# Retention heads by tokens: group norm along the free axis, samples read from split old states

## What is computed

```
S_new = g * S_old + k^T v            # per head and sample: 256 x 512, stored
o     = q S_new                      # prompt: (decayed scores) v
o     = (o - mean(o)) * rsqrt(var(o) + eps) * gn_gain     # over the 512 channels of a token
ret   = (silu(gate) * o) @ w_ret_out
```

## Time and profile before

| | us |
|---|---|
| median of three runs | 2689.16 |
| lowest and highest | 2684.42, 2693.64 |
| the profiled execution | 2686.85 |
| its span, first to last instruction | 2685.0 |
| TensorE busy in it | 2561.6 |
| VectorE busy | 1396.5 |
| GpSimd busy | 1422.3 |
| ScalarE busy | 629.4 |

### The profile page before, as it was taken

The page is one execution under the profiler, slowest core; times in us unless marked ns, Lnnn a source line. Parts: engine busy times, 40 slices in busy tenths (PEclk is TensorE's granted clock), DMA queues, the critical chain, the costliest instruction groups (busy, mean ns, idle before and its releaser), DMA issues.

```text
span 2685.0 us, 52601 instructions
## 1 busy us (share of the span) xinstructions
PE 2561.6 (95%) x20388; PEld 2521.4 (94%) x20388; DVE 1396.5 (52%) x1480; ACT 629.4 (23%) x925; POOL 1422.3 (53%) x845
## 2 busy tenths in 40 slices
PE   6999999999999999999999999999999999999997
PEld 6999998989899999999988989999998999999997
DVE  7664636468864553133365455454787645430333
ACT  2312121216651121001112031312266411110111
POOL 4252535346666656566642525252566666566654
PEclk9999999999999999999998999999999999999999
DMA  4445353522233322332334353535222333223222
GB/s 152 166 126 169 122 173 115 172 69 93 75 92 95 91 88 90 89 94 87 95 125 162 118 159 122 165 122 173 81 83 77 97 89 93 87 86 102 86 87 86
DMA packets 113046, 298.97 MB, mean 111 GB/s; under 512 B 11680, under 2 KB 12448, under 8 KB 112864
## 3 DMA queue, kind: packets, MB, share of 16 engines
q1 hardware_dynamic: 60480, 199.78, 24.2%
q10 hardware_dynamic: 52384, 96.56, 10.6%
HBM read 255.92 MB, written 40.38 MB: 110 GB/s over the span
## 4 chain that ended last, share of the span: by engine, by line
PE 69%; DVE 12%; DVEq 6%; issue 3%; ACT 3%; DMA 3%; ACTq 2%; POOL 1%; POOLq 1%
PE proj L325 42%; PE aux L325 20%; PE aux L531 3%; DVE scratch L943 2%; DVEq L1087 2%; DMA scratch<-in_sret 2%; DVEq L946 1%; PE aux L522 1%; DVE scratch L896 1%; PE aux L512 1%; POOL w_low L313 1%; DMA out_ret_s<-scratch 1%; PE aux L479 1%; DVE scratch L901 1%; ACTq L1387 1%
## 5 line engine op out<-in xcount | busy, mean ns | idle before, releaser
L311 POOL TENSOR_SCALAR w_high<-w_raw 128x1024 fp32r<-128x1024 f32 (+3 forms) x420 | 442.1, 1053 | 1177.5 <-PE proj L325 946.5
L313 POOL TENSOR_TENSOR w_low<-w_raw,w_high 128x1024 fp32r<-128x1024 f32 (+3 forms) x420 | 979.7, 2333 | 62.2 <-issue 2.9
L325 PE MATMUL proj<-x_high,w_high 128*128 128x260 f32 x3072 | 637.7, 289 | 59.6 <-DVE scratch L791 15.8
L325 PE MATMUL proj<-x_high,w_low 128*128 128x260 f32 x3072 | 626.7, 286 | 0.0
L325 PE MATMUL proj<-x_low,w_high 128*128 128x260 f32 x3072 | 626.4, 286 | 0.0
L325 PEld LDWEIGHTS proj<-x_high,w_high 128*128 128x128 f32 x3072 | 483.0, 192 | 68.5 <-issue 28.0
L325 PEld LDWEIGHTS proj<-x_low,w_high 128*128 128x128 f32 x3072 | 481.8, 192 | 0.0
L325 PEld LDWEIGHTS proj<-x_high,w_low 128*128 128x128 f32 x3072 | 481.3, 192 | 0.0
L325 PE MATMUL proj<-split_scratch,w_high 128*128 128x260 f32 x2368 | 383.8, 284 | 4.7 <-DVE ret_acc L720 2.0
L325 PEld LDWEIGHTS proj<-split_scratch,w_high 128*128 128x128 f32 x2368 | 325.2, 189 | 7.7 <-DVE ret_acc L720 5.0
L325 PE MATMUL aux<-split_scratch,w_high 128*128 128x260 f32 x1632 | 265.3, 285 | 5.9 <-DVE scratch L978 3.8
(11 more groups left out here) (167 smaller groups left out, 2726.2 us busy)
## 6 DMA issues: line engine op xcount, KB each, us to landing
w_raw<-in_wstream SPq DMA_DIRECT2D x252, 512.0 KB, 3.5
scratch<-in_sret ACTq DMA_DIRECT2D x64, 512.0 KB, 6.4
out_ret_s<-scratch ACTq DMA_DIRECT2D x64, 512.0 KB, 6.3
w_raw<-in_wstream SPq DMA_DIRECT2D x72, 448.0 KB, 3.3
w_raw<-in_wstream SPq DMA_DIRECT2D x48, 384.0 KB, 3.1
scratch<-v_rows ACTq DMA_DIRECT2D x64, 256.0 KB, 4.9
w_raw<-in_wstream SPq DMA_DIRECT2D x48, 320.0 KB, 2.8
out_ret_p<-scratch ACTq DMA_DIRECT2D x8, 512.0 KB, 3.0
```

Of the source, the lines that this page charges most:

```text
L311: pool.tensor_scalar(WH[:, j, w], WR[:, j, w], 1.0, 0.0, ALU.mult, ALU.add)
L313: pool.tensor_tensor(WL[:, j, w], WR[:, j, w], WH[:, j, w].bitcast(F32), ALU.subtract).then_inc(s["w_split"], 1)
L325: m = pe.matmul(out, wt[:, w, blk * P:(blk + 1) * P], x[xi], start=first and n == 0, stop=last and n == 2)
```

## The change

Attention is computed by token blocks: the split scores are the stationary operand and the split values move, so that an output tile has 128 tokens on the partitions and 512 channels along the free axis. Group norm then works along the free axis: VectorE takes mean and variance with `bn_stats` and `bn_aggr` from the accumulator, ScalarE takes the root, VectorE the reciprocal and the shift on one column, ScalarE normalises. In the next head, after its two query units, TensorE transposes the normalised tiles back to channels (`turned_back`, 16 blocks and 4 small ones); VectorE multiplies them by the gate (`read_back`), ScalarE and VectorE split the result (`gated_out`, `og_split`). `og_split` moves from behind VectorE's first reading of a query tile to behind the rotation of k. The column sums are gone.

The samples are read out of their old states: ScalarE and VectorE split a state into SSH and SSL (`state_high`, `state_low`), and TensorE multiplies the split states, moving, by split query columns of which all but two are zero (`read_out`, 4 matmuls of 512 columns a sample), summing all samples in one accumulator. `samples` adds the parts, decays them and adds the q-k product times v. The first four read-outs stand behind the value units, the others between and behind the last gate units.

The gate tiles are in natural order, the four accumulators for these uses get another order with one semaphore each, the ring of v rows has four places instead of two, and in a first head the series moves ahead of and between the value tiles.

```diff
-                    rotate(0, QF, new_gain)
-                    rotate(KT, KF, lambda: low(QL, QF, QH, 1.0, 1))
+                    rotate(0, QF, lambda: None)
+                    if not first:
+                        read_back(hh - 1)
+                    dve.wait_ge(s["sfin_st"], hh * 16 + 16)
+                    rotate(KT, KF, q_parts)
                     ts(KSC[:], KF[:, :, SEQ:TOK], DK ** -0.5, None, ALU.mult)
-                    if not first:
+                    if first:
+                        series_begin()
+                        state_terms()
+                        state_low(0)
+                    else:
+                        new_gain()
                         for m_ in range(MT):
                             ret_add(tb, QK, m_)
...
+                def turned_back(hh):
+
+
+                    for use in TOKENS:
+                        pe.wait_ge(*turn(hh, use))
+                    for e in range(VT):
+                        if e == VT - 1:
+                            for c in range(VT):
+                                m = pe.transpose(AUX[:, BANK["OTS"], c * NS:(c + 1) * NS], NOS[:, c * P:(c + 1) * P],
+                                                 ID[0:NS, 0:NS])
+                            m.then_inc(s["aux_mm"], 1)
+                        aux_begin(hh, f"OT{e}")
+                        for t in range(TT):
+                            m = pe.transpose(aux(f"OT{e}")[:, t * P:(t + 1) * P], NO[:, t, e * P:(e + 1) * P], ID[:])
+                        m.then_inc(s["aux_mm"], 1)
...
+                    else:
+                        for i in range(KT):
+                            whole(ub, i, tb, i, XH, XL)
+                        turned_back(hh - 1)
+                    for i in range(KT, QK):
+                        whole(ub, i, tb, i, XH, XL)
                     if not first:
                         ret_out(hh, ub, QK, tb, QK)
...
+                        for d in range(KT):
+                            pe.wait_ge(s["s_low"], hh * (NS * KT) + (b * KT + d + 1))
+                            for n, part in enumerate((SSH, SSL)):
+                                m = pe.matmul(aux("RO", 2 * NS), QP[:, d, b, :], part[:, d, :],
+                                              start=b == d == n == 0, stop=b == NS - 1 and d == KT - 1 and n == 1)
+                            m.then_inc(s["ro_done"], 1)
...
                     gate(1)
-
-
-                    sample_out(0)
-                    gate(3, midway=lambda: sample_out(1))
-                    sample_out(2)
+                    gate(2)
+                    read_out(4)
+                    gate(3)
+                    read_out(5)
                     pe.wait_ge(s["kv_low"], hh * (2 * TT) + 2 * TT)
                     pe.wait_ge(s["st_low"], hh * TT + TT)
-                    for e in range(VT):
-                        attend(e)
-                        sample_out(3 + e)
+                    attend(3)
                     final_state(0)
-                    sample_out(NS - 1)
+                    read_out(6)
+                    attend(2)
+                    attend(1)
+                    read_out(7)
                     final_state(1)
-                    pe.wait_ge(s["gn_sum"], hh * 2 + 1)
-                    column_sums(tb, v0 + VT + T_MEAN, SUM)
-                    gate(2)
-                    pe.wait_ge(s["gn_sum"], hh * 2 + 2)
-                    column_sums(tb, v0 + VT + T_VAR, SUM)
+                    aux_begin(hh, "SEL")
+                    attend(0)
+                    samples()
...
+                    scaled(3)
+                    next_state(4)
+                    store_state(2)
+                    silu(1)
+                    scaled(4)
+                    next_state(5)
+                    store_state(3)
+                    scaled(5)
+                    next_state(6)
+                    state_high(4)
                     silu(2)
+                    store_state(4)
```

More of the change, by code:

```diff
@@ L241, in build @@
         v_ld = [sem(f"vb_loaded{j}") for j in range(VRING)]
+        a_free = [sem(f"aux_free{j}") for j in range(BANKS)]
         r_free = [sem(f"ring_free{j}") for j in range(RING)]
@@ L260, in freed, with turn, aux @@
             return r_free[n % RING], layer * USES[n % RING] + (n // RING + 2)
+        def turn(hh, use):
+            return a_free[BANK[use]], hh * BANK_USES[BANK[use]] + (TURN[use] + 2)
+        def aux(use, rows=P):
+            return AUX[0:rows, BANK[use], :]
         def slot(idx):
@@ L399, in spread @@
                 return q
[L401 to L406, removed]
             def norm_sums(outs, signal):
@@ L418, in _ @@
             pe.sem_inc(s["w_used"], 2)
-            for done in r_free:
+            for done in r_free + a_free:
                 pe.sem_inc(done, 1)
@@ L442, in x_early, with aux_begin @@
                 def x_early(t):
-                    whole(ub0, B_X_EARLY + t, tb0, C_X_EARLY + t, XH, XL,
-                          variances=(layer + 1) * HEADS if t == 1 else None)
+                    whole(ub0, B_X_EARLY + t, tb0, C_X_EARLY + t, XH, XL)
+                def aux_begin(hh, use):
+                    done, count = turn(hh, use)
+                    pe.wait_ge(done, count - 1)
+                def turned_back(hh):
[11 more added lines that the diff above has]
+                        m.then_inc(s["aux_mm"], 1)
                 def one_head(head, first):
@@ L482, in one_head @@
                         m.then_inc(s["aux_mm"], 1)
+                    aux_begin(hh, "QK")
+                    for d in range(KT):
+                        m = pe.matmul(aux("QK", NS)[:, 0:NS], KSC[:, d, :], QF[:, d, SEQ:TOK],
+                                      start=d == 0, stop=d == KT - 1)
+                    m.then_inc(s["aux_mm"], 1)
                     for i in range(TT // 2):
-                        aux_begin(N_TK + i)
+                        aux_begin(hh, f"TK{i}")
                         for j in range(2):
@@ L564, in _ @@
                     one_head(head, False)
-                for t in range(X_EARLY):
-                    x_early(t)
+                x_early(0)
+                turned_back((layer + 1) * HEADS - 1)
+                x_early(1)
                 ret_out((layer + 1) * HEADS, ub0, B_X_EARLY + X_EARLY, tb0, C_X_EARLY + X_EARLY)
```

393 lines of the change are left out of this document (227 added, 166 removed).

## The result

The changed kernel takes 2764.3 us (median of four runs, 2760.33 to 2766.02) against 2686.79 for the kernel before (also four): ratio 1.0301, 95% interval 1.0278 to 1.0325, slower (these two medians alone give 1.0289). The forecast was 2765 in 2718 to 2798. The profiled execution took 2766.02, its span is 2764.2, 79.2 more than before.

What follows compares the result with a forecast made beforehand. TensorE, busy 95% of the span, was taken as the bound. Work and waits saved were outweighed by new stops: two layers of a first head +11.1, three later heads +9.1 each and layer end +0.5, +78 on 2686.85, gave 2765, range 2718 to 2798.

Steps and rivals of the forecast that it cites:

- Stop 1: Turn back after the query units: fourth transposed block waits for VectorE's read behind the query's second rotation; 1.8 of wait.
- Stop 2: Output product after the last key unit waits for VectorE's late split of the gated output: 3.85 plus 1.0, 4.9.
- first heads' read-out 0: In a layer's first head, read-out 0 waits for VectorE's lambda series and convolution terms: 5.7, and 1.5 of clock.
- stop 4: Sample 4's read-out, between third and fourth gate units, waits for its state's ring slot: 10.0, plus 1.5 of clock.
- stop 3: A transposed value block, moved to the first key transposes' bank, waits for VectorE's two subtractions: 0.9.
- smaller stops: State 6's read-out, the last read-out and the samples' sum wait for VectorE: 2.5 a head (0 to 5).
- the head's start 1.5: At the loop's turn only a 2.66 idle time remains, so the clock holds and a later head gains 1.5.
- Rival (a): The clock falls at the turn back and before the output product too: 21 more, 2786; chance 0.17.
- +20.2 for the first two heads of a layer: Net sums of gains, losses and stops: first head +11.1, later head +9.1.
- 8 x 1.89 = 15.1 of read-outs: One-column read-outs of eight samples leave TensorE's queue, 15.1 less work per head.
- (b): Rival: the state's round trip is short, transfers near 3.7, 8 x 4.4 less: 2730; chance 0.13.
- (c): Rival: sample 4's read-out finds its state ready, 2673; decides under 1.8 a head of wait and clock; chance 0.07.

Runs made afterwards that it cites:

- the ring's order: Kernel with all edits, old states' ring put in one order on TensorE, ScalarE and VectorE, gated output rounded ahead of the query: 2603.84 us, ratio 0.9702 to the kernel before.

## Why the prediction was right, point by point

**The direction and the mechanism.** Right. The chain new state, store, load, copy, split of a ring slot ends behind TensorE's three gate units, and the stops eat what TensorE's lists gained. Stops 1 and 2 and the first heads' read-out 0 have an experiment each that removes them; stop 4 has one that shortens it, one that moves it to read-out 5, and the ring's order, which leaves 1.5 of it; stop 3 and the smaller stops have none.

**The stops.** Stop 1: 1.8 of wait said, 2.13 found. Stop 2: 3.85 of wait and 1.0 of pacing by VectorE said; 3.78 of wait found, and no pacing: the four splits take 0.89 each, not 1.25, and no idle time stands inside the output product. In the place of the 1.0 came the 1.2 of fallen clock, which was not in the sum. Stop 3: 0.9, found 1.01. Stop 4: wait 10.0, found 9.76 to 10.99 in the eight heads. Smaller stops 2.5, found 1.7. First head's read-out 0: 5.7, found 5.59. The waits were sums of durations from the earlier trace rows, each along one engine's list to the instruction that is waited for. The splits of stop 2, in VectorE's order of time:

```profile
334.12 3.55 DVE L765 SCALAR_TENSOR_TENSOR split_scratch<-scratch,gn_cur,split_scratch 128x520 fp32r<-128x520 f32 x4
```

**The clock, misread.** "the head's start 1.5, since only 2.66 is left there, under the 3.78 that kept the clock": this step failed. I read only the first record behind each idle time of the earlier trace rows. The records that follow there, in the kernel before, show that neither 1.74 nor 3.78 kept the clock (a pair of 260 columns takes 0.40 at 2.4 GHz and 0.64 at 1.2 GHz):

```profile
573.82 0.64 PE L325 MATMUL proj<-split_scratch,w_low 128*128 128x260 f32 x2
...
689.60 0.62 PE L325 MATMUL proj<-x_high,w_high 128*128 128x260 f32 x2
```

Behind 3.78 the clock fell 0.8 after the restart at 688.79; behind 1.74 it was down by the second record, and the first, 0.90, is one of four matmuls, not of a pair. In the changed kernel the clock falls behind the loop's turn, 2.37 to 2.43, in four places of four, behind stop 2, 3.77 or 3.78, in six of six, and behind stop 1, 2.13, in five of six; it holds behind each of 1.01 (stop 3) and 1.38 (a smaller stop). So two query units take 13.80 instead of 11.54: the 1.5 did not come, and 0.8 were lost on top. Rival (a), whose 3.78 "(held)" is the same misreading, came true beside the forecast: behind stop 1 the key units take 1.5 more, behind stop 2 the output product 1.2. A later head is 14.1 longer in layer 0 (153.66 against 139.54), not 9.1. Head start 2.3, stop 1 with its clock 1.9, stop 4 with its read-out at 1.2 GHz 1.2, stop 2 by its removal 0.8 are 6.2 more; the smaller stops give 0.8 back, and the sum is 14.5, of which 14.1 came.

**Why the total still came out.** By luck: errors of both signs. The forecast has +20.2 for the first two heads of a layer. Here are their windows, before:

```profile
37.95:280.03 242.08, 229.34 (x1768) 222.23 (x1769) 144.63 (x177) 54.60 (x84) 98.62 (x52) 0.97 0.43 142
...
1357.28:1612.72 255.44, 241.25 (x1769) 232.88 (x1769) 144.48 (x177) 54.80 (x84) 98.64 (x52) 0.93 0.42 136
```

And in the changed kernel, with the later heads behind them:

```profile
36.09:299.71 263.62, 223.70 (x1560) 201.28 (x1561) 148.10 (x235) 77.47 (x131) 98.05 (x52) 0.92 0.40 131
299.71:453.37 153.66, 132.22 (x934) 121.16 (x935) 73.31 (x111) 39.30 (x67) 59.37 (x32) 0.92 0.39 129
1403.15:1665.50 262.35, 221.73 (x1561) 199.35 (x1561) 149.19 (x235) 77.41 (x131) 98.10 (x52) 0.93 0.40 132
1665.50:1818.65 153.15, 131.76 (x934) 120.65 (x935) 73.44 (x111) 39.46 (x67) 59.41 (x32) 0.93 0.39 129
```

Layer 0 gives +21.5, as said. Layer 1 gives only +6.9, because the same two heads before took 13.4 more there than in layer 0, at a clock of 0.93. TensorE's order of time in the kernel before shows where, a read-out of 3.57 instead of 1.89 and an attention block of 3.76 instead of 2.10, both half clock:

```profile
1434.71 3.57 PE L531 MATMUL aux<-scratch 128*128 128x1 f32 x16
...
1438.15 3.76 PE L512 MATMUL aux<-split_scratch 128*128 128x512 f32 x12
```

The sum was built on one head of layer 0 and took every other for its copy. So 12 too much here, 8 too little in the next head of the two layers and 5 in the rest: 79.2 instead of 78. Had the clock of the later heads been read rightly, and nothing else changed, the sum would have been some 30 higher (six heads, 5 each), about 2795, farther from what was measured.

**The removed work.** "8 x 1.89 = 15.1 of read-outs" was counted as free to win. In the kernel before it is not: there, only 54 of 93 come back. For this change the count can stand, since its read-outs no longer wait for new states; that is argued, no run shows it.

**Rivals.** (b), a short round trip, did not occur: store to load is 6.69, near the 7.25 taken, and that load landed after 6.6, near the 6.4 taken. (c) did not either; its point of decision bears out in kind, for in the kernel with the ring in one order read-out 4 starts at once, and with the other stops cut too it is faster than before by 3.0%.

**The rule on transposes.** Stop 1 is 1.8 us of transposes, 2.13 of wait and 0.4 of transposes. Behind it the clock fell in five heads of six; in the sixth (from 1530.92) the same wait left the key units at 11.76. With the same transposes and no wait it held in all six. The Trainium skill ("TensorE: Matmul & The Clock Gate", Part 4: PE-mode transpose) says that transposes don't count as busy in the same way. By that rule stop 1 is one idle stretch of 4.3, and behind 3.78 of plain idle time the clock fell too, so these runs agree with it. But it also fell behind 1.74 and behind 2.4 of plain idle time, so the 2.13 of wait can be enough without the rule. The runs do not decide; real matmuls in the place of the transposes were not tried.

**What stays open.** Why layer 1's first heads ran at a lower clock before, why an idle time near 2 us let the clock fall in some places and not in others, and what holds the last 1.3 us at the output product.

## What to carry to other kernels

A state that goes through a ring of slots is on time or late by where its copies, splits and reloads stand in each engine's list: put the reload's wait behind what another engine is already waiting for, and use one order on all engines. Here the order of the engines' lists, changed in five places, turned +3% into -3% with the same arithmetic and transfers; the ring's order was 61 of those 160 us. When the work leaves the bound engine, list each place where it will then arrive too early, and price the half clock behind each stop with it: keeping TensorE busy in three of the stops gave 28 us back. How much of the 77 us of slowdown was clock is not known, since the kernel before had stretches at half clock too (0.975 granted over its span, 0.964 after). And read the clock behind an idle time from the records that follow, not from the first alone.

## What was not expected of the hardware

The clock need not be down at the first matmul behind an idle time for it to fall. Behind 2.42 at the loop's turn in layer 0 it was down from the first record (299.71 above). Behind 2.37 at the same place in layer 1 the first three pairs ran at 2.4 GHz, and it fell 1.1 us after the restart:

```profile
1665.50 0.50 PE L346 MATMUL proj<-x_high,w_high 128*128 128x260 f32 x2 [2.37 <-issue]
...
1666.60 0.64 PE L346 MATMUL proj<-x_low,w_high 128*128 128x260 f32 x2
```

Ahead of both stand the same small float32 products of the samples; what sets the delay was not found.

A matmul of 512 columns costs the same with 16 stationary columns as with 128. In the changed kernel the four of a read-out take 0.92 to the next instruction, 0.23 each, and the 12 of the scores' product behind it 2.73 (to 435.11), 0.23 each:

```profile
431.46 1.09 PE L509 MATMUL aux<-split_scratch,q_pairs 128*16 128x512 f32 x4
432.38 2.88 PE L563 MATMUL aux<-split_scratch 128*128 128x512 f32 x12
```

Mean and variance of 512 PSUM elements on 128 partitions take VectorE 0.70 and 0.18; the first is the 0.70 of a plain pass, as the prediction took it:

```profile
435.31 0.70 DVE L960 BATCH_NORM_STATS2 norm_stats<-aux 128x6 f32<-128x512 f32 x1 [1.48 <-PE aux L563]
436.08 0.18 DVE L962 BATCH_NORM_AGGREGATE norm_mean_var<-norm_stats 128x2 f32<-128x6 f32 x1
```
